# Two modulation units and two weight blocks of the prologue loaded by feature columns, and the first FFN products made chunk by chunk

## The reference, cut to what matters

```
def adaln(cond, w, b):
    m = jax.nn.silu(cond) @ w + b                       # w: (1024, 9 * 1024)
    return [t[:, None, :] for t in jnp.split(m, N_MOD, axis=-1)]

def ffn_sublayer(x, shift, scale, gate, g_pre, g_post, w_in, w_out):
    h = modulate(rmsnorm(x, g_pre), shift, scale)       # x * (1 + scale) + shift
    a, b = jnp.split(h @ w_in, 2, axis=-1)              # w_in: (1024, 2 * 2816)
    h = (jax.nn.silu(a) * b) @ w_out
    return x + FFN_RES * gate * rmsnorm(h, g_post)
```

## Time and profile before

| | us |
|---|---|
| median of 3 runs (lowest to highest) | 3013.35 (3012.11 to 3014.33) |
| the profiled execution, its own time | 3015.84 |
| span of the profiled execution, first to last instruction | 3014.0 |
| TensorE busy in the span | 2957.3 (98%) |
| VectorE, ScalarE, GpSimd busy | 2207.0, 1153.1, 564.2 |
| read from HBM | 510.37 MB |
| last slab of `ada_first` in, by the chain of waits | about 30.3 |
| first product of block 2 (f = 1), by the same chain | 48.9 |

### The profile page before, as it was taken

One profiled execution on the slowest core, in us unless ns is written; L12 is line 12 of the kernel. 1 busy time (PEld: TensorE's weight loads), 2 busy tenths in 40 slices (PEclk: granted clock), 3 DMA queues, 4 the chain that ended last, 5 costly groups with the idle time before them and its releaser, 6 DMA issues.

```text
span 3014.0 us, 46617 instructions
## 1 busy us (share of the span) xinstructions
PE 2957.3 (98%) x18194; PEld 2748.1 (91%) x18194; DVE 2207.0 (73%) x2897; ACT 1153.1 (38%) x1966; POOL 564.2 (19%) x586
## 2 busy tenths in 40 slices
PE   7999999999999999999999999999999999999999
PEld 6999888999999998999899999979999999889998
DVE  6888678887987656888888576768888888775444
ACT  4222664223322424222422365543224222664222
POOL 1111212112111212111211144631112111211001
PEclk9999999999999999999999999999999999999999
DMA  8667436665665445766566443337665666333443
GB/s 299 210 213 216 146 84 193 211 211 170 215 213 175 116 131 173 226 211 197 185 214 192 134 118 105 97 95 236 211 209 184 216 211 200 108 81 113 127 128 96
DMA packets 589696, 517.76 MB, mean 172 GB/s; under 512 B 66773, under 2 KB 523046, under 8 KB 587686
## 3 DMA queue, kind: packets, MB, share of 16 engines
q1 hardware_dynamic: 588918, 514.53, 56.6%
q10 hardware_dynamic: 560, 0.25, 0.0%
HBM read 510.37 MB, written 4.33 MB: 171 GB/s over the span
## 4 chain that ended last, share of the span: by engine, by line
PE 89%; issue 4%; DVE 2%; POOL 2%; ACT 1%; DMA 1%; SPq 0%; another core or an unknown queue 0%; DVEq 0%; POOLq 0%; ACTq 0%
PE bank L1698 19%; PE bank L1700 18%; PE bank L1699 18%; PE bank L1749 9%; PE bank L1748 9%; PE bank L1747 9%; PE bank L1715 2%; PE bank L1722 1%; PE bank L619 1%; PE bank L644 1%; DMA ada_first<-w_ada 1%; PE bank L1780 0%; POOL small L2379 0%; POOL small L2384 0%; POOL hg_kr L1497 0%
## 5 line engine op out<-in xcount | busy, mean ns | idle before, releaser
L1698 PE MATMUL bank<-h_hi,w_hi 128*128 128x384 f32 x3328 | 1120.7, 337 | 0.0
L1700 PE MATMUL bank<-h_hi,w_lo 128*128 128x384 f32 x3328 | 1114.6, 335 | 0.0
L1699 PE MATMUL bank<-h_lo,w_hi 128*128 128x384 f32 x3328 | 1113.7, 335 | 0.0
L1934 ACT ACTIVATE w_hi<-raw 128x1024 fp32r<-128x1024 f32 x646 | 680.6, 1062 | 1022.8 <-PE bank L1700 481.8
L2090 DVE TENSOR_TENSOR w_lo<-raw,w_hi 128x1024 fp32r<-128x1024 f32 x648 | 811.1, 1275 | 310.6 <-ACT w_hi L1934 305.4
L1698 PEld LDWEIGHTS bank<-h_hi,w_hi 128*128 128x128 f32 x3328 | 625.3, 188 | 11.0 <-ACT tmp L1953 1.6
L1699 PEld LDWEIGHTS bank<-h_lo,w_hi 128*128 128x128 f32 x3328 | 625.4, 188 | 6.1
L1700 PEld LDWEIGHTS bank<-h_hi,w_lo 128*128 128x128 f32 x3328 | 625.1, 188 | 0.0
L2117 DVE SCALAR_TENSOR_TENSOR fold<-ada_raw,cond,fold 128x1024 f32<-128x1024 f32 x462 | 616.4, 1390 | 0.1
L2420 POOL TENSOR_TENSOR h_lo<-tmp,h_hi 128x384 fp32r<-128x384 f32 x176 | 249.3, 1416 | 1758.7 <-DVE h_hi L2161 1758.7
L1749 PE MATMUL bank<-w_hi,h_lo 128*128 128x512 f32 x1056 | 414.0, 392 | 0.0
(11 more groups left out here) (204 smaller groups left out, 2445.9 us busy)
## 6 DMA issues: line engine op xcount, KB each, us to landing
raw<-w_ffn_in SPq DMA_DIRECT2D x352, 512.0 KB, 5.0
ada_raw<-w_ada SPq DMA_DIRECT2D x264, 512.0 KB, 4.2
raw<-w_ffn_out SPq DMA_DIRECT2D x176, 512.0 KB, 4.7
raw<-w_hgrn_in SPq DMA_DIRECT2D x40, 512.0 KB, 4.1
g_rows<-g_dram SPq DMA_DIRECT2D x12, 1024.0 KB, 7.0
raw<-w_attn_qkv SPq DMA_DIRECT2D x24, 512.0 KB, 5.4
raw<-w_conv_in SPq DMA_DIRECT2D x24, 512.0 KB, 5.0
ada_first<-w_ada SPq DMA_DIRECT2D x16, 512.0 KB, 10.5
```

What stands on the lines that cost most here:

```text
L1698: mm(out, wh, h_hi[:, k, :], start=(k == 0), stop=False)
L1699: mm(out, wh, h_lo[:, k, :], start=False, stop=False)
L1700: last = mm(out, wl, h_hi[:, k, :], start=False, stop=(k == DC - 1))
L1934: A(w_hi[:, b % RING, :], raw[:, b % RAW, :], ACT.Copy).then_inc(w_hi_made, 1)
```

## The change

The 16 slab loads and the loads of blocks 0 and 1 become five loads by feature columns: chunks (0, 1), (2, 3), (4, 5), (6), (7), a chunk being 128 features. A load of two chunks brings, for unit 1 and for unit 0, all 1024 rows by 256 columns of `w_ada` (1 MB each, in runs of 1 KB), and the rows of w_in for these features from blocks 0 and 1 (128 KB each, runs of 512 B). The two last loads bring one chunk (512 KB twice, 64 KB twice, runs of 512 B). SP issues them behind the constants and y; blocks 2 and 3 follow. For each chunk, TensorE makes 16 matmuls of 128 columns, ScalarE copies one 128 x 256 tile, TensorE makes two matmuls by a new constant `sel_sum` (which turns to columns and sums the four row groups at once), VectorE makes the gain and the shift in two small instructions, ScalarE modulates in place (`hf`, two instructions), VectorE rounds 384 columns, GpSimd makes their low part, and TensorE makes four products with `h_hi` and two with `h_lo`. `w_hi` and `w_lo` of blocks 0 and 1 are made per load. The unread matmuls, `first_tile` and `first_blocks` of sublayer 0 are gone.

```diff
+        def first_load(i):
+            c, w = first_loads[i]
+            for n, u in enumerate((1, 0)):
+                src = W["w_ada"][0, :, u * D + c * P:u * D + (c + w) * P].rearrange("(k p) n -> p k n", p=P)
+                sp.dma_start(ada_first[i][n][:, :, :], src).then_inc(ada_first_in[i], 16)
+            for j in range(2):
+                sp.dma_start(raw[:, j, c * P:(c + w) * P].rearrange("p (k n) -> p k n", n=P),
+                             blocks[j][:, c:c + w, :]).then_inc(ada_first_in[i], 16)
...
-        first_slabs(range(3))
-        sp.dma_start(base_k[:, :], ins["k_base"]).then_inc(consts_in, 16)
+        sp.dma_start(base_k[:, 0:P + 10], ins["k_base"]).then_inc(consts_in, 16)
...
-        first_slabs(range(3, 5))
...
-        first_slabs(range(5, 2 * DC))
-        for b in range(4):
+        for i in range(len(first_loads)):
+            first_load(i)
+        for b in range(2, 4):
             load_block(b)
...
-                sp.wait_ge(ada_used, 1)
+                sp.wait_ge(ada_used, DC)
```

TensorE, in place of `ada_half`, `ada_turn`, the unread matmuls, `first_tile(0)` and `first_blocks(0)`:

```diff
+        def rows_of(c):
+            i = load_of(c)
+            at = (c - first_loads[i][0]) * P
+            pe.wait_ge(ada_first_in[i], 4 * 16)
...
+                pe.wait_ge(rows_copied, c - 1)
+            for r in range(2):
+                for q in range(4):
+                    for n in range(2):
+                        last = mm(psum[c % 2][32 * q:32 * q + 32, n * P:(n + 1) * P], cond[:, 4 * r + q, :],
+                                  ada_first[i][n][:, 4 * r + q, at:at + P], start=(r == 0 and n == 0),
+                                  stop=(r == 1 and n == 1), tile_position=(0, 32 * q), skip_group_check=True)
+            last.then_inc(ada_used, 1)
+        def columns_of(c):
+            pe.wait_ge(rows_copied, c + 1)
...
+            for n in range(2):
+                last = mm(psum[2 + c % 2][:, 2 * n:2 * n + 2], chunk_rows[c % 2][:, n * P:(n + 1) * P], sel_sum,
+                          start=True, stop=True)
+            last.then_inc(ada_turned, 1)
+        def chunk_high(c):
+            pe.wait_ge(first_lo, load_of(c) + 1)
+            pe.wait_ge(chunk_hi, c + 1)
+            for j in range(2):
+                for w in (w_hi, w_lo):
+                    mm(psum[6 + j][:, 0:T], w[:, j, c * P:(c + 1) * P], h_hi[:, c, :], ...
+        def chunk_low(c):
+            pe.wait_ge(chunk_lo, c + 1)
+            for j in range(2):
+                last = mm(psum[6 + j][:, 0:T], w_hi[:, j, c * P:(c + 1) * P], h_lo[:, c, :], ...
+        for t in range(NT):
+            turn_normed(0, t)
+        for i, (c0, w) in enumerate(first_loads):
+            for c in range(c0, c0 + w):
+                rows_of(c)
+            for c in range(c0, c0 + w):
+                columns_of(c)
+            if w == 1 and i < len(first_loads) - 1:
+                continue
+            for c in range(c0 - (w == 1), c0 + w):
+                chunk_high(c)
+                chunk_low(c)
```

ScalarE (`chunks`, after the squares and the copies of the transposed tiles), and the end of its boundary 0:

```diff
+            for c in range(c0, c0 + w):
+                act.wait_ge(ada_used, c + 1)
+                need(act, ada_turned, c - 1)
+                A(chunk_rows[c % 2][:, :], psum[c % 2][:, 0:2 * P], ACT.Copy).then_inc(rows_copied, 1)
+            act.wait_ge(ada_first_in[i], 4 * 16)
+            A(w_hi[:, 0:2, cols], raw[:, 0:2, cols], ACT.Copy).then_inc(first_hi, 1)
...
+            for c in range(c0, c0 + w):
+                act.wait_ge(cols_made, c + 1)
+                for g, ts in enumerate((slice(0, 1), slice(1, NT))):
+                    last = A(hf[:, ts, c, :], hf[:, ts, c, :], ACT.Identity, bias=mod[:, c, g:g + 1],
+                             scale=s_cols[:, c, g:g + 1])
+                last.then_inc(chunk_modulated, 1)
...
+                act.wait_ge(first_hi, len(first_loads))
+                act.sem_inc(w_hi_made, 2)
```

VectorE (`chunks`) and the end of its boundary 0; GpSimd's part:

```diff
+            for c in range(c0, c0 + w):
+                dve.wait_ge(ada_turned, c + 1)
+                gain = norm_col(0, 0) + c
+                V.tensor_scalar(s_cols[:, c, :], psum[2 + c % 2][:, 0:2], scale_bias[:, c:c + 1],
+                                g_cols[:, gain:gain + 1], ALU.add, ALU.mult)
+                V.tensor_scalar(mod[:, c, :], psum[2 + c % 2][:, 2:4], b_cols[:, c:c + 1], None,
+                                ALU.add).then_inc(cols_made, 1)
+            dve.wait_ge(first_hi, i + 1)
+            V.tensor_tensor(w_lo[:, 0:2, cols], raw[:, 0:2, cols], w_hi[:, 0:2, cols].bitcast(F32),
+                            ALU.subtract).then_inc(first_lo, 1)
+            for c in range(c0, c0 + w):
+                dve.wait_ge(chunk_modulated, c + 1)
+                V.tensor_copy(h_hi[:, c, :].rearrange("p (t n) -> p t n", t=NT), hf[:, :, c, :]).then_inc(chunk_hi, 1)
...
+                dve.wait_ge(first_lo, len(first_loads))
+                dve.sem_inc(w_lo_made, 2)
...
+                for c in range(DC):
+                    gp.wait_ge(chunk_hi, c + 1)
+                    G.tensor_tensor(h_lo[:, c, :].rearrange("p (t n) -> p t n", t=NT), hf[:, :, c, :],
+                                    h_hi[:, c, :].rearrange("p (t n) -> p t n", t=NT).bitcast(F32),
+                                    ALU.subtract).then_inc(chunk_lo, 1)
```

More of the change, by code:

```diff
@@ L356, in loop, with load_of @@
             body(i)
-    put = pool_of((ring_at, ring_end), (x_at, span[0]), span_rest, (h_at, h_end))
-    ada_first = [put(f"ada_first{n}", [P, D]) for n in range(2 * DC)]
+    put = pool_of((ring_at, ring_end), (x_at, span[0]), span_rest, (ring_end, ring_end + 2 * D * 4),
+                  (span[0], span[0] + 2 * D * 4))
+    def load_of(c):
+        return next(i for i, (c0, w) in enumerate(first_loads) if c0 <= c < c0 + w)
+    first_loads = ((0, 2), (2, 2), (4, 2), (6, 1), (7, 1))
+    ada_first = [[put(f"ada_first{c}_{n}", [P, DC, w * P]) for n in range(2)] for c, w in first_loads]
     vin = put("vin", [P, 6, P])
+    put = pool_of((free_at, end_of_sbuf))
+    chunk_rows = [put(f"chunk_rows{z}", [P, 2 * P]) for z in range(2)]
+    scale_bias = put("scale_bias", [P, DC])
     VEC_ROWS = (128, 128, 32, 128, 64, 113)
@@ L1841, in ffn @@
                 if f == 0:
[L1842 removed]
+                    if s > 0:
+                        first_blocks(s, (6, 7))
                 else:
@@ L1893, in _ @@
         pe.wait_ge(cond_made, 3)
[L1894 to L1915, removed]
+        def rows_of(c):
+            i = load_of(c)
+            at = (c - first_loads[i][0]) * P
+            pe.wait_ge(ada_first_in[i], 4 * 16)
+            if c < 2:
+                pe.wait_ge(turn_copied_a if c == 0 else turn_copied_v, 3 + 1)
+            else:
+                pe.wait_ge(rows_copied, c - 1)
[6 more added lines that the diff above has]
+            last.then_inc(ada_used, 1)
@@ new lines, in columns_of @@
+        def columns_of(c):
+            pe.wait_ge(rows_copied, c + 1)
+            if c < 2:
+                pe.wait_ge(turn_copied_a if c == 0 else turn_copied_v, 3 + 2)
+            else:
+                pe.wait_ge(cols_made, c - 1)
+            for n in range(2):
[7 more added lines that the diff above has]
+                for w in (w_hi, w_lo):
+                    mm(psum[6 + j][:, 0:T], w[:, j, c * P:(c + 1) * P], h_hi[:, c, :], start=(c == 0 and w is w_hi),
+                       stop=False, skip_group_check=True)
@@ L2042, in boundary @@
             else:
[L2043 to L2052, removed]
+                for t in range(NT):
+                    y_squares(e, t)
+                for t in range(NT):
+                    act.wait_ge(hn_turned, 2 * t + 1)
+                    A(hf[:, t, 0:4, :].rearrange("p k n -> p (k n)"), psum[2 * t][:, :], ACT.Copy).then_inc(turn_copied_a, 1)
+                for i in range(len(first_loads)):
+                    chunks(i)
+                act.wait_ge(chunk_modulated, DC)
+                act.sem_inc(hf_low, NT)
+                act.sem_inc(hf_high, NT)
+                act.wait_ge(first_hi, len(first_loads))
+                act.sem_inc(w_hi_made, 2)
             if e < N_SUB:
```

88 lines of the change are left out of this document (49 added, 39 removed).

## The result

The changed kernel takes 3030.65 us (median of 4 runs, 3027.78 to 3034.09) against 3013.84 for the kernel before (4 runs): a ratio of 1.0054, with a 95% interval of 1.0042 to 1.0066. That is 16.8 us slower. The profiled executions differ by 16.9 us: 3032.72 against 3015.84. All the times compared in this document are of runs in the chip's faster state.

What follows compares the result with a forecast made beforehand. TensorE, 98% busy, was taken as the bound, so only block 2's start counts: 48.9 to 56.7 us (+7.8) plus clock +2.2 gives +10, 3025.8 us (3023.4 against the median); range 3012 to 3032.

Steps and rivals of the forecast that it cites:

- the clock: TensorE's slow stretches in the loop's first pair and around the wait before block 2: +2.2 us, between nothing and 5.9.
- ScalarE's waits for the DMA of blocks 4 and 5: Sign of being right: ScalarE idle before its roundings of blocks 4 and 5, released by the DMA of `raw`.
- the idle queue: Sign of being right: the load queue idle around 48 us.
- the landings: Sign of being right: the five loads land up to 40 us (18.4, 25.3, 32.2, 36.3 and 40.3).
- Block 2 at 56 to 60: Sign of being right: TensorE's first product of block 2 at 56 to 60 us.
- GpSimd's 1.4 us: Sign of being right: GpSimd's low parts in the loop take 1.4 us each.
- TensorE idle before `chunk_low`: Sign of being right: in the loop, TensorE waits ahead of the low products of a chunk.
- Transfer: Loads by columns: 1 KB runs at 349 GB/s (bounds 291 and 410), 28.8 us together, last landing at 40.3 us.
- The loop: Chunk loop starts at 19; three pairs of 7.8 us end at 42.4, chunks 6 and 7 add 6.1, release at 48.5.
- The new wait: Blocks 4 and 5 load only after the release at 48.5; block 2 starts 8.2 us behind it, at 56.7.
- the rival of a slow clock all the way: TensorE stays at 0.50 through the loop, pairs take 10.3 us, block 2 at 66: +20, 3033 us; chance 0.12.
- The rival of overlap: The loop's pairs overlap at 5.2 us with landings by 36, block 2 at 48.9: no change, 3013.4 us; chance 0.20.

Runs made afterwards that it cites:

- the long runs: The changed kernel with the parts of w_ada read in 8 KB and 4 KB runs (same bytes, other values): 3028.36 us, ratio 1.0055 to the kernel before.
- the loop was mended: The changed kernel with Silu ahead of blocks 4 and 5, early slot release and next load's rows ahead of products: 3016.27 us; with long w_ada runs too, 3011.69.
- the three profiles of the loop as it was: The changed kernel (3030.65 us), it with the Silu ahead of blocks 4 and 5 (3020.07), and it with sixteen unread matmuls in the wait (3030.69).
- The first experiment: The changed kernel with sublayer 0's roundings and low parts of blocks 4 and 5 behind the Silu and product of f = 0: 3020.07 us, ratio 1.0020.
- the five profiles with the Silu behind block 5: The changed kernel (3030.65 us) and it with early slot release (3025.76), long w_ada runs (3028.36), TensorE's order changed (3023.90) or sixteen unread matmuls (3030.69).
- the kernel with the joined load: The changed kernel with Silu moved, early release and TensorE's order changed, plus the first two loads joined into one of four chunks: 3019.34 us, ratio 1.0027.
- the first group: The first four experiments (Silu moved, early release, long w_ada runs, TensorE's order changed); the kernel before, timed beside them, had a median of 3012.98 us.

## Why the prediction was right, and where its terms were off

The sign and the cause were right: a loop strung together by TensorE's program order, and the wait for the Silu behind block 5. The size was short: +10 forecast, +16.8 measured. That is 0.8 outside the +5 to +16 to which the forecast gave 0.60, and it is luck that the time still lies in the range up to 3032, with 1.35 us to spare: two of the four runs are above it (3032.72 and 3034.09). The term that was mis-sized most is the clock. Of the signs that were named, ScalarE's waits for the DMA of blocks 4 and 5, the idle queue (SP issued nothing from 38.2 to 49.6) and the landings came true. Block 2 at 56 to 60 did not (62.75), nor GpSimd's 1.4 us (1.01), nor TensorE idle before `chunk_low`: its waits in the loop are for VectorE's rounding, before `chunk_high` (5.1 us in three waits). By its steps:

**Transfer.** 349 GB/s for 1 KB runs was taken from a line between two rows; 345 was measured in the changed kernel. The last load was in at 40.8 us where 40.3 was forecast. The estimate from the Trainium skill (DMA: Bandwidth & Descriptors, "Why small descriptors are slow (HBM only)") was 383 for 1 KB, and the measurement decides against it: the overhead per run is larger here than the page's 3 cycles. The claim that the loop and not the transfer sets the end holds: the long runs changed nothing alone, and about 3 us once the loop was mended.

**The loop.** It starts at 19.85 (19 forecast): y was in at 10.15, earlier than the 11 assumed, but squares and transposes then took 9.7 us in place of 7.85. Its three pairs took 25.8 us where the sum had 23.4; chunks 6 and 7 took 8.1 to the release (45.62 to 53.70) where it had 6.1. A pair at full clock was sized well (7.8 forecast, 7.4 seen), but by errors that partly cancel: GpSimd 1.01 in place of 1.42, against VectorE's rounding 0.55 in place of 0.36 and slower modulation, 1.86 per pair in place of 1.6. That TensorE's program order strings the pairs together was right: reordering alone moved the release to 46.3, by 4.0 to 7.4 us against the three profiles of the loop as it was. The tail was sized too short even without the clock: 7.1 us at a clock of 0.94 for 6.1. I let chunk 7 follow chunk 6 more closely than ScalarE allows, which copies the rows of 7 only after it has modulated 6.

**The new wait.** 8.2 us forecast from release to block 2, 9.05 measured: block 5 was in 7.5 us after the release (53.70 to 61.24), where I had 6.5 for the three transfers together, and rounding and Silu took 1.5 for my 1.7. TensorE waited for the Silu as described. The first experiment shows that this was the largest single cost: it took some 10 us off the median, 6 to 7 of them the edit's own by block 2's distance from the release (2.3 us there, 8.4 to 9.4 in the five profiles with the Silu behind block 5).

**The sum of these.** At full clock the forecast start of block 2 was 56.7. The start adds 0.85, the pairs take 1.3 off (three of 7.36 for 23.4), the tail adds 1.0 and the wait 0.85: 58.1. The clock adds 3.7 in the pairs (25.8 for 22.1) and 1.0 in the tail (8.08 for 7.09): 62.8, measured 62.75.

**The clock, the term that failed.** I had +2.2 for all of it, "between nothing and 5.9". Measured it is 4.7 us in the loop and 2.2 behind block 2 (the 4.7 us at 0.50 right after the wait, and the 2.2 us lost by the first product of w_out), 6.9 together and above my upper bound. Without the clock the change would have cost 9.2 us where I had 7.8. Of its parts, the one I named for the first pair (+2.5) hardly came: the rows of that pair took 2.0 us, as at full clock, and 5.2 us of transposes without a gap stand right before them, which I had overlooked. The slow stretches came later, in all three pairs and the tail, where I had put nothing. The Trainium skill's rule on the clock (TensorE: Matmul & The Clock Gate, "HAM oscillation — how this bites in real kernels") has bursts between waits for DMA each start slow. The trace agrees in part: the bursts in this loop wait for other engines, and it shows stretches of 1.00 and of 0.50 in turn (0.90, 0.72, 0.87 and 0.71 in the mean). So the rival of a slow clock all the way was half true, and its 3033 lay nearer than my 3023.

**The rival of overlap.** Its condition was a pair of 5.2 us and landings by 36. Neither was met. With TensorE's order changed the chunks did overlap, and with the wait gone as well the result was its "no change", but by another way: the landings were as late as before.

## What to carry to other kernels

When buffers are released only at the end of a stage, look at which engine has to consume the next fill in program order before it does what the bottleneck waits for: here two roundings of blocks nobody needed yet stood ahead of the one Silu that TensorE needed. A loop over chunks pays only if the engine that begins each chunk does so before it finishes the one before; otherwise its stages add up. A finer transfer that makes shorter runs is dear only when it is the pace of the stage, so first find what hides it. And where TensorE works in bursts with waits between, the clock belongs in the sum with its own rows: here it was 7 of 17 us.

## What the runs showed of the hardware

The rate against the length of a run is now measured at four points on one queue, each in windows of one microsecond: 288 to 291 GB/s at 512 B, 345 at 1 KB, about 389 at 2 KB (from the kernel with the joined load) and 410 at 4 KB. A row of that kernel:

```profile
14.00:15.00 1.00, 0.53 (x3) 0.56 (x4) 1.00 (x3) 0.00 (x0) 0.75 (x1) 1.00 1.06 389
```
A straight line in time per run through 512 B and 4 KB (28 and 160 ns) gives 47 ns at 1 KB and 85 at 2 KB, thus 349 and 387.

GpSimd's subtraction of 128 x 384 took 1.01 us in the loop, where VectorE was mostly idle, and 1.42 in the rest of the kernel, where VectorE is busy; that the two are linked was not tested. With the same instructions ahead of it, the release differed by 3.4 us between profiles, most of it with the granted clock, so a change of a prologue is read from several profiles or from distances between events rather than from one start time. The spread between whole runs goes with the clock too: of the 13 runs of the kernel before in the first group, the fastest (3007.58 us) had a mean granted clock of 0.999, and the three at 0.994 took 3016.36 to 3017.09.
